# First feed-forward of a two-block transformer kernel: silu one step later on ScalarE, the gated product behind the first residual addition, the P5 copy ahead of a rounding

## The reference, cut to what matters

```python
h = rmsnorm(x, norm_ffn[l])
x = x + (jax.nn.silu(h @ w_gate[l]) * (h @ w_up[l])) @ w_down[l]
```

## Time and profile before

| | |
|---|---|
| median of 3 runs | 2567.9 us (2567.16 to 2567.9) |
| the profiled execution | 2567.3 us, of which span 2565.7 us |
| TensorE matmul busy | 2526.1 us (98%) |
| VectorE busy | 1843.5 us (72%) |
| ScalarE busy | 1300.5 us (51%) |
| mean granted TensorE clock | 0.997 |
| first feed-forward, iterations | about 462 to 1120 us, 65.2 us each |

### The profile page before, as it was taken

How to read it: one execution, slowest core, us unless ns; L and a number is a source line. 1 busy time by engine, 2 the same in 40 slices (tenths; PEclk the granted TensorE clock), 3 DMA queues, 4 the chain that set the end, 5 groups by cost and what they waited for, 6 DMA issues and landing times.

```text
span 2565.7 us, 28052 instructions
## 1 busy us (share of the span) xinstructions
PE 2526.1 (98%) x11526; PEld 2089.5 (81%) x11526; DVE 1843.5 (72%) x1526; ACT 1300.5 (51%) x1240; POOL 6.2 (0%) x15
## 2 busy tenths in 40 slices
PE   8999999999999999999999999999999999999998
PEld 7888888788888888888888888888888888888886
DVE  5565577788888888867544554554789999999996
ACT  6544555444455444545444554333565555555554
POOL 0000000000000000000000000000000000000000
PEclk9999999999999999999999999999999999999999
DMA  8455446655555555555545555565556555555552
GB/s 282 157 168 193 136 148 214 210 189 192 196 197 191 190 193 190 187 189 197 174 156 195 170 169 192 191 197 195 175 202 205 195 195 196 195 195 194 193 194 96
DMA packets 239615, 480.50 MB, mean 187 GB/s; under 512 B 7632, under 2 KB 7760, under 8 KB 239232
## 3 DMA queue, kind: packets, MB, share of 16 engines
q1 hardware_dynamic: 238496, 474.10, 55.1%
q0 software_dynamic: 992, 4.60, 0.5%
HBM read 476.57 MB, written 2.10 MB: 187 GB/s over the span
## 4 chain that ended last, share of the span: by engine, by line
PE 95%; ACT 2%; DVE 2%; issue 1%; DMA 0%; SPq 0%; DVEq 0%; ACTq 0%
PE acc L609 24%; PE acc L613 24%; PE acc L611 24%; PE misc L609 6%; PE misc L613 6%; PE misc L611 6%; PE misc L642 2%; ACT w_hi L1013 2%; DVE x L1467 1%; DVE hid L1798 0%; PE misc L726 0%; PE misc L706 0%; DMA x<-in_x 0%; PE misc L720 0%; DVE w_lo L1440 0%
## 5 line engine op out<-in xcount | busy, mean ns | idle before, releaser
L1440 DVE TENSOR_TENSOR w_lo<-w_raw,w_hi 128x2048 fp32r<-128x2048 f32 x407 | 929.4, 2287 | 364.0 <-ACT w_hi L1013 362.5
L1013 ACT ACTIVATE w_hi<-w_raw 128x2048 fp32r<-128x2048 f32 x407 | 778.7, 1916 | 494.9 <-PE acc L613 378.0
L609 PE MATMUL acc<-w_hi,xt_hi 128*128 128x512 f32 x1456 | 576.9, 396 | 3.6 <-ACT hid L1016 3.3
L613 PE MATMUL acc<-w_hi,xt_lo 128*128 128x512 f32 x1456 | 568.4, 390 | 0.0
L611 PE MATMUL acc<-w_lo,xt_hi 128*128 128x512 f32 x1456 | 567.7, 390 | 0.0
L609 PEld LDWEIGHTS acc<-w_hi,xt_hi 128*128 128x128 f32 x1456 | 273.9, 188 | 62.6 <-ACT hid L1016 3.7
L613 PEld LDWEIGHTS acc<-w_hi,xt_lo 128*128 128x128 f32 x1456 | 273.8, 188 | 58.1
L611 PEld LDWEIGHTS acc<-w_lo,xt_hi 128*128 128x128 f32 x1456 | 274.1, 188 | 55.4
L1440 DVE TENSOR_TENSOR w_lo<-w_raw_more,w_hi 128x2048 fp32r<-128x2048 f32 x101 | 230.9, 2286 | 76.2 <-ACT w_hi L1013 75.8
L1013 ACT ACTIVATE w_hi<-w_raw_more 128x2048 fp32r<-128x2048 f32 x101 | 193.5, 1916 | 148.4 <-PE acc L613 79.0
L609 PE MATMUL misc<-w_hi,xt_hi 128*128 128x512 f32 x640 | 250.0, 391 | 0.0
(11 more groups left out here) (264 smaller groups left out, 3080.7 us busy)
## 6 DMA issues: line engine op xcount, KB each, us to landing
w_raw<-in_w_in SPq DMA_DIRECT2D x136, 1024.0 KB, 5.1
w_raw<-in_w_ffn_up SPq DMA_DIRECT2D x60, 1024.0 KB, 5.0
w_raw<-in_w_up SPq DMA_DIRECT2D x33, 1024.0 KB, 5.1
w_raw<-in_w_out SPq DMA_DIRECT2D x32, 1024.0 KB, 5.1
w_raw<-in_w_down SPq DMA_DIRECT2D x30, 1024.0 KB, 7.2
w_raw_more<-in_w_ffn_up SPq DMA_DIRECT2D x28, 1024.0 KB, 5.1
w_raw<-in_w_ffn_down SPq DMA_DIRECT2D x28, 1024.0 KB, 6.5
w_raw<-in_w_gate SPq DMA_DIRECT2D x27, 1024.0 KB, 5.2
```

Source lines behind the costliest of these rows:

```text
L609: nc.tensor.matmul(bank, hi[:, j, :], w_hi[:, t % RING, j, :], start=first and j == 0, stop=False, skip_group_check=shared)
L613: end = nc.tensor.matmul(bank, lo[:, j, :], w_hi[:, t % RING, j, :], start=False, stop=last and j == C - 1, skip_group_check=shared)
L1013: nc.scalar.activation(w_hi[:, t % RING], raw_tile(steps[t].slot), ACT.Copy).then_inc(hi_ready, 1)
L1440: nc.vector.tensor_tensor(w_lo[:, t % RING], raw_tile(steps[t].slot), w_hi[:, t % RING].bitcast(F32), ALU.subtract).then_inc(lo_ready, 1)
```

## The change

On ScalarE, P1's copy waits for `hid_ready` in place of `hid_turned`, so for the product in `hid` itself and not for its transpose. In the first iteration the two `ht_hi` pieces (`hid_hi(0)`) move from before P5's copy to U2, behind U2's split. The silu of the first half of `gate` moves from step P2 to step P4, that of the second half from P4 to D0; in both steps it stands behind that step's split. On VectorE, `gated_sums` moves from step D0, where it stands between the split and the addition of D0, to the head of step D1, ahead of that step's split. No operation is added or taken away, and the loads and TensorE's program stay the same.

```diff
@@ products_read (ScalarE)
             if name == "P1":
                 act.wait_ge(tile_used, t + 1)
-                act.wait_ge(hid_turned if ffn == 1 else ua_turned, i)
+                act.wait_ge(hid_ready if ffn == 1 else ua_turned, i)
                 copy(dst_a[:, 0, :], acc[:, 0, 0, :], scale[:, 0:1]).then_inc(p1_copied, 1)
@@ ScalarE, iterations of the first feed-forward
                 split(t + LEAD)
-                if i == 1 and name == "P5":
+                products_read(1, i, t, name, gate, hid)
+                if i == 1 and name == "U2":
                     hid_hi(0)
-                products_read(1, i, t, name, gate, hid)
-                if name == "P2":
+                if name == "P4":
                     silu_gate(i, 0)
-                if name == "P4":
+                if name == "D0":
                     silu_gate(i, 1)
@@ VectorE, iterations of the first feed-forward
                 t = iteration_t(1, i) + k
+                if name == "D1":
+                    gated_sums(i)
                 split(t + LEAD)
                 if i == 1 and name == "U2":
                     hid_lo(0)
                 results_read(1, i, t, name, gate, hid)
-                if name == "D0":
-                    gated_sums(i)
                 if name[0] == "D":
                     add_group(t, ("ffn1_down", i - 1, int(name[1])))
```

## The result

The changed kernel takes 2544.2 us (median of 6 runs, 2543.8 to 2544.8) against 2566.8 us for the kernel before (6 runs, 2565.6 to 2567.9). The ratio is 0.9912, with a 95% interval of 0.9900 to 0.9925: 22.5 us less. The forecast was 2545 us, from a sum of 22.4 us.

The account below looks back on a forecast made before the run. TensorE was taken as the bound, busy 2526.1 of 2565.7 us. Savings of 15.6 (D2's stalls), 0.8 (last iteration) and 6.0 (first iteration) make 22.4 us off the profiled 2567.3: forecast 2545 us, range 2541.5 to 2550.

Parts of the forecast that it names:

- the steady part: First feed-forward: D2's wait goes in nine iterations, 15.6 us, and the last iteration's transpose wait, 0.8 us.
- the first iteration: P5's copy comes in time for U2's second half, so idle and half-rate matmuls go: 6.0 us.
- The stall of D2: Between D1 and D2 TensorE waits for D0's late addition: 1.73 us in each of nine iterations, all to go.
- gated product behind the addition: On VectorE the 1.22 us product runs after D0's addition, at no cost, with 8.5 us of cover.
- The 4.0 us of the addition: Time to spare between the end of D0's addition (647.3) and D2's possible start (651.34).
- the 0.75 us ahead of it: VectorE is free, after w_lo of D3, 0.75 us before D0 ends.
- The 0.9 us of ht_lo: First iteration: VectorE's ht_lo empties banks 0 and 1 at 478.4, G2 is due at 479.3; the thinnest cover.
- the 5.98 us: First iteration's loss at U2's second half: 3.25 us idle plus 12 matmuls at 1.2 GHz, expected to go whole.
- A: First iteration keeps part of its loss: G2 waits 1.3 us for ht_lo and the clock falls; 2549 us, chance 0.10.
- B: Something else ends just as late before D2, so only the first iteration gains; 2561 us, chance 0.04.
- C: Nothing moves: D2 really waits for a weight load or its w_lo; 2567 us, chance 0.02.
- D: Slower: VectorE lacks time, w_lo late at P1 with idle and clock fall, 6.0 us each; 2599 us, chance 0.01.

Follow-up runs that it names:

- fillers: Changed kernel plus two VectorE reductions of 128x2048 with unused results in each iteration, in front of D0's addition: 2546.0 us.
- the late ht_lo: Changed kernel with VectorE's `hid_lo(0)` of the first iteration at P6 in place of U2, behind one more w_lo: 2548.9 us, again 2548.1.
- three fillers: Changed kernel plus three unused VectorE reductions of 128x2048 in each iteration, in front of D0's addition: 2578.1 us, again 2577.3.

## Why the prediction was right

**The sum.** 22.4 us were forecast and 22.5 measured. That it fits within 0.1 us is partly luck: the steady part came out 0.3 us above its term and the first iteration 0.3 us below, and both differences are within the noise. The forecast of 2545 counted down from one execution of 2567.3 us; from the median of six runs, 2566.8, the same sum gives 2544.4.

**The stall of D2.** Right in size and in place. 9 x 1.73 + 0.83 = 16.4 us were forecast; the silus alone brought 16.7. The chain worked out from the rows was met to about 0.1 us: VectorE free 0.75 us ahead of D0's end (0.79 measured), an iteration of 63.5 us (63.47). The prediction took silus and product together and did not say that the first silu alone would do; that one, or both, give the same time without the product. The second silu alone was not run. The part called "gated product behind the addition" has no share of its own in the result. What it gives is distance: the addition no longer has the 1.22 us product ahead of it.

**The covers.** The 4.0 us of the addition and the 0.75 us ahead of it were tested with fillers. 4.6 us fit, with about 0.2 us to spare; 6.9 us do not, and bring back an idle of 1.96 us. The 0.9 us of ht_lo were met in the profile after (479.03 to 479.92; all rows of the first iteration stand 0.64 us later there than before, as 474.25 for 473.61 shows, and less that they meet the forecast's 478.4 and 479.3), and the late ht_lo turned them into 2.92 us of idle.

**The first iteration.** 6.0 us forecast, 5.7 and 5.6 measured alone. The reason given was the block of ScalarE at P1, together with the pieces ahead of the copy. The first is the cause. The second is not needed: moving the pieces alone gains nothing that can be told, and P1's wait alone gains all.

**The clock.** That the fall would go with the idle was right, but the 5.98 us hold about 2.6 us that are not a fixed price: after the same idle of 3.25 us it was 12 or 13 slow matmuls in three profiles and 7 and 6 in two more, at 0.20 us more for each, so 1.2 to 2.6 us. A median of 5.7 against 6.0 fits that. The prediction states bounds of 3.4 to 6.2 us for this part, but its range was added up with 5.3 to 6.2, and it gives no working for the 5.3. With a fall of only six matmuls the loss is 3.4 + 1.2 = 4.6 us, below that end. The prediction also reads that 1.2 GHz shows only from the 3.25 us idle on. The granted clock says so. But the first eight transposes of the kernel before take 1.94 us (from 6.68), where eight such take 1.03 us in the last iteration after the change and 1.97 us behind the 3.09 us idle in the second profile with three fillers. So TensorE was slow at the start too, and the column of the granted clock does not show it.

**The rivals.** A: the idle at G2 did not come, the cover held. B and C: no wait of D2 is left. D: no w_lo is late at P1, neither after the change nor with three fillers, whose stall comes at D2. Its bound for a slower kernel, a mean loss over 2.5 us in the nine iterations, fits what they did: their mean is 3.2 us (28.6 / 9), and the kernel is 10.5 us slower than before.

## What to carry to other kernels

Where two engines prepare operands in turn and each executes in order, look for an operation that waits for the other engine's result just ahead of an operation that doesn't; swapped, both waits shrink (here 3.09 to 0.37 us), and one such swap was enough (that of the first silu). Work out how much each cover holds before counting parts of a change: moving the product on top of that brought nothing. Let a wait name what it needs: P1's copy writes over `gate`, which the product reads last, and waiting for the product and not for the transpose behind it did what the reordering was meant to do. Once an engine is the bound, an idle can cost twice its length: with three fillers 1.96 us cost 2.23 us and, with a fall, 1.7 us more.

## What the runs showed of the hardware

In the first feed-forward, the granted clock of TensorE fell after idles of 1.96 us in ten of eighteen cases (two profiles), after one of 2.28 us, after two of 3.09 and 3.10 us, and after all five of 3.25 us; after 2.92 us it did not fall in two profiles, and after the 1.47 us stalls of D2 in none of 45 (nine in each of five profiles). So from 1.96 to 2.92 us the idle's length alone doesn't tell. The Trainium skill (TensorE: Matmul & The Clock Gate, Part 1: The HAM clock gate) says that the activity window runs free of the program, and that the moment of the change moves with it; the two profiles of the three fillers fit that, with the same idles and a fall in the odd iterations of one, and in the first and the even ones of the other. The same page (HAM oscillation — how this bites in real kernels) ties the fall to longer idles than some of these; here 1.96 us was enough, and the measurement decides. A fall cost 1.7 us in the kernel with three fillers, and 1.2 to 2.6 us behind the 3.25 us idle.

VectorE operations of 2.29 us that follow each other start every 2.20 us (631.05 and 633.25 in the profile after; to 633.91, with the gate sum of 0.74 between, it is 2.86, not 3.02). So the durations of rows in a chain add up to about 0.08 us a row more than the chain takes.
